# A float32 diffusion step on one core: VectorE's order in the Strassen cycles of the MLPs rewritten, one weight sum stored elsewhere, one strip a product later

## What is computed

```
h = rmsnorm(x, norm_g[layer, 1]) * (1 + sc2) + sh2
x = x + g2 * (jnp.square(jax.nn.relu(h @ mlp_w1[layer])) @ mlp_w2[layer])
```

## Time and profile before

| | |
|---|---|
| median of 3 runs | 1557.08 us (1556.45 to 1558.0) |
| the profiled execution, its own time | 1556.89 us |
| its span | 1555.1 us |
| TensorE (PE) busy | 1518.0 us, 98% |
| weight loads (PEld) | 1477.0 us, 95% |
| VectorE (DVE) | 1139.8 us, 73% |
| ACT | 684.3 us, 44% |
| GpSimd (POOL) | 629.7 us, 40% |
| DMA queue 1 | 159.34 MB, 32.0% of 16 engines' span |

### The profile page before, as it was taken

How to read it: one execution, slowest core, us unless ns; L and a number is a source line. 1 busy time by engine, 2 the same in 40 slices (tenths; PEclk the granted TensorE clock), 3 DMA queues, 4 the chain that set the end, 5 groups by cost and what they waited for, 6 DMA issues and landing times.

```text
span 1555.1 us, 28369 instructions
## 1 busy us (share of the span) xinstructions
PE 1518.0 (98%) x11754; PEld 1477.0 (95%) x11754; DVE 1139.8 (73%) x1877; ACT 684.3 (44%) x1140; POOL 629.7 (40%) x410
## 2 busy tenths in 40 slices
PE   8999999999999999999999999999999999999998
PEld 7999999999999999999999999999999999999998
DVE  5338678675774787887797888773584698889886
ACT  5323333344442354445355434662442355445553
POOL 0233313314322464665574253101333476567641
PEclk9999999999999999999999999999999999999999
DMA  9454334213233334433535122001222212331222
GB/s 328 160 184 149 115 110 130 96 62 109 82 128 119 112 118 162 147 111 123 177 95 162 35 79 65 28 1 55 82 68 68 82 55 73 104 95 55 81 83 82
DMA packets 123168, 162.20 MB, mean 104 GB/s; under 512 B 4640, under 2 KB 87584, under 8 KB 123040
## 3 DMA queue, kind: packets, MB, share of 16 engines
q1 hardware_dynamic: 121808, 159.34, 32.0%
q10 hardware_dynamic: 1232, 1.05, 0.2%
HBM read 156.44 MB, written 3.93 MB: 103 GB/s over the span
## 4 chain that ended last, share of the span: by engine, by line
PE 72%; DVE 15%; ACT 6%; issue 3%; SPq 2%; DMA 2%; POOL 0%; DVEq 0%; ACTq 0%
PE ps L745 42%; PE ps L1169 19%; DVE fx L2602 3%; PE ps L864 3%; PE ps L1417 2%; DVE held L2616 2%; PE ps L1365 1%; ACT wH L1479 1%; DVE fq L2576 1%; DMA ada<-in_ada_w 1%; SPq L573 1%; DVE ps L2106 1%; PE ps L1001 1%; DVE u L2593 1%; PE ps L1034 1%
## 5 line engine op out<-in xcount | busy, mean ns | idle before, releaser
L2031 POOL TENSOR_TENSOR wL<-raw,wH 128x512 fp32r<-128x512 f32 x188 | 288.0, 1558 | 668.2 <-ACT wH L1461 511.2
L1169 PE MATMUL ps<-fx,wH 128*128 128x320 f32 x1120 | 250.6, 312 | 13.5 <-DVE held L2616 8.7
L745 PE MATMUL ps<-hH,wH 128*128 128x320 f32 x704 | 221.1, 314 | 1.9 <-DVE hL L2117 1.3
L745 PE MATMUL ps<-hH,wL 128*128 128x320 f32 x704 | 217.6, 309 | 0.0
L745 PE MATMUL ps<-hL,wH 128*128 128x320 f32 x704 | 217.5, 309 | 0.0
L1169 PEld LDWEIGHTS ps<-fx,wH 128*128 128x128 f32 x1120 | 185.7, 188 | 21.8 <-issue 14.4
L2031 POOL TENSOR_TENSOR wL<-raw_high,wH 128x512 fp32r<-128x512 f32 x100 | 141.8, 1449 | 115.0 <-ACT wH L1461 115.0
L1169 PE MATMUL ps<-fx,wL 128*128 128x320 f32 x560 | 173.1, 309 | 0.0
L745 PE MATMUL ps<-wH,hH 128*128 128x256 f32 x560 | 162.1, 289 | 2.4 <-DVE hL L2117 2.1
L745 PE MATMUL ps<-wL,hH 128*128 128x256 f32 x560 | 158.3, 283 | 0.0
L745 PE MATMUL ps<-wH,hL 128*128 128x256 f32 x560 | 158.3, 283 | 0.0
(11 more groups left out here) (302 smaller groups left out, 3872.6 us busy)
## 6 DMA issues: line engine op xcount, KB each, us to landing
ada<-in_ada_w SPq DMA_DIRECT2D x40, 1024.0 KB, 5.4
raw<-in_mlp_w SPq DMA_DIRECT2D x64, 512.0 KB, 3.7
raw_high<-in_mlp_w SPq DMA_DIRECT2D x64, 512.0 KB, 3.8
raw<-in_even_w_in SPq DMA_DIRECT2D x28, 512.0 KB, 6.1
pre_w<-in_ada_w SPq DMA_DIRECT2D x16, 512.0 KB, 8.9
raw<-in_odd_w_qkv SPq DMA_DIRECT2D x10, 512.0 KB, 3.6
raw<-in_even_w_out SPq DMA_DIRECT2D x8, 512.0 KB, 3.7
raw<-in_odd_w_o SPq DMA_DIRECT2D x6, 512.0 KB, 3.4
```

The lines of the kernel that those rows point to most:

```text
L745: last = nc.tensor.matmul(ps[:, bank, 0:width], a_, b_, start=(k == 0 and p_ == 0), stop=(k == nk - 1 and p_ == 2))
L1169: last = nc.tensor.matmul(ps[:, bank, 0:HALF], a_, b_, start=(opens and k == 0 and p_ == 0), stop=(k == nk - 1 and p_ == 2), skip_group_ch ...
L2031: last = nc.gpsimd.tensor_tensor(wL[:, at % 4, cs], source(key)[:, cs], wH[:, at % 4, cs].bitcast(F32), ALU.subtract)
```

## The change

Nothing is added to or taken from the arithmetic; four things move.

1. `strassen_cycle`: VectorE's list of one cycle in another order.
2. `source`, `wait_raw_free`, `add_blocks`: T4's sum of the first matrix is written over B21's raw buffer instead of `t24_first`. It stands behind `t_lo(s, B21)`, the buffer's next load waits for T4's low part, and the second matrix's T3 sum (into `t24_first`) waits for T2's low part and T4's sum instead of T4's low part.
3. `first_strassen`: the middle strip (`part(1)`) stands behind T1's products instead of T3's.
4. Last cycle: the two row halves of the `mlp_w2` block are loaded in swapped order and `F_AT` follows, so k = 0, 1 are the features of F11 and F21, k = 2, 3 those of F22 and F12.

```diff
@@ F_AT
-    return k % 2 + ((2, 0) if k > 1 else (4, 6))[half]
+    return k % 2 + ((4, 6) if k > 1 else (2, 0))[half]
@@ source
             if key[0] in ("p", "q") and key[2] in (T2, T4):
+                if key[0] == "p" and key[2] == T4:
+                    return raw(key[:2] + (B21,))
                 return (t24_first if key[0] == "p" else t24_second)[:]
@@ wait_raw_free
-            wait_low(engine, *key)
+            wait_low(engine, *(key[:2] + (T4,) if key[0] == "p" and key[2] == B21 else key))
@@ w2
-                        halves = [mlp_w2[layer, 512 * c + 256 * j:512 * c + 256 * (j + 1), 512 * tile:512 * (tile + 1)]
+                        halves = [mlp_w2[layer, 512 * c + 256 * (1 - j):512 * c + 256 * (2 - j), 512 * tile:512 * (tile + 1)]
@@ first_strassen
                     one(T3, S3, 6 + m, m, False)
-                part(1)
                 wait_low(pe, "p", s, T1)
                 pe.wait_ge(dve_free, v)
                 for m in range(2):
                     one(T1, S1, m, m)
+                part(1)
@@ add_blocks
                         if which == "q":
-                            wait_low(dve, "p", WINO * layer_ + n, T4)
+                            wait_low(dve, "p", WINO * layer_ + n, T2)
+                            wait_source(dve, ("p", WINO * layer_ + n, T4))
...
+                    elif which == "p":
+                        wait_low(dve, which, s, B21)
+                        out, a, b, op = b21, b21, t2, ALU.subtract
@@ strassen_cycle
                     t_lo(s, B22)
+                    t_lo(s, B21)
                     p_add(s, T4)
-                    t_lo(s, B21)
+                    q_add(s2, T3)
+                    combine(c, F11, 0)
+                    q_add(s2, T2)
+                    combine(c, F11, 1)
                     t_lo(s, T4)
-                    combine(c, F11, 0)
-                    q_add(s2, T3)
-                    combine(c, F11, 1)
+                    combine(c, F21, 0)
+                    q_add(s2, T1)
+                    combine(c, F21, 1)
+                    operand_lo(c, A11_)
                     modulate(c, 1)
-                    q_add(s2, T2)
-                    combine(c, F21, 0)
-                    operand_lo(c, A11_)
-                    combine(c, F21, 1)
-                    q_add(s2, T1)
                     combine(c, F22, 0)
+                    combine(c, F22, 1)
                     operand_sum(c, S3_)
-                    combine(c, F22, 1)
+                    operand_sum(c, S2_)
                     q_add(s2, T4)
-                    operand_sum(c, S2_)
-                    operand_sum(c, S1_)
                     operand_lo(c, S2_)
...
@@ last_cycle
                     t_lo(s, B22)
-                    p_add(s, T4)
                     held_out(2)
                     t_lo(s, B21)
+                    p_add(s, T4)
                     held_out(3)
```

More of the change, by code:

```diff
@@ L2648, in strassen_cycle @@
                     q_add(s2, T4)
-                    operand_sum(c, S2_)
-                    operand_sum(c, S1_)
                     operand_lo(c, S2_)
-                    product_out(c, 0, 0)
-                    product_out(c, 0, 1)
+                    for m in range(4):
+                        product_out(c, 0, m)
                     operand_lo(c, S3_)
-                    product_out(c, 0, 2)
-                    product_out(c, 0, 3)
-                    product_out(c, 1, 0)
+                    for m in range(3):
+                        product_out(c, 1, m)
@@ L2658, in strassen_cycle @@
                     operand_lo(c, A22_)
-                    product_out(c, 1, 1)
-                    operand_sum(c, S4_)
-                    product_out(c, 1, 2)
                     product_out(c, 1, 3)
                     product_out(c, 2, 0)
-                    operand_lo(c, S1_)
+                    operand_sum(c, S1_)
                     for m in range(1, 4):
                         product_out(c, 2, m)
+                    operand_lo(c, S1_)
+                    operand_sum(c, S4_)
@@ L2667, in strassen_cycle @@
                     product_out(c, 3, 0)
+                    product_out(c, 3, 1)
                     operand_lo(c, S4_)
-                    for m in range(1, 4):
-                        product_out(c, 3, m)
+                    product_out(c, 3, 2)
+                    product_out(c, 3, 3)
                     for m in range(4):
```

## The result

| | before | the change |
|---|---|---|
| median, runs side by side | 1556.78 us (4 runs) | 1546.56 us (4 runs, 1545.89 to 1546.95) |
| ratio | | 0.9932, 95% interval 0.9915 to 0.9950 |
| span of the profiled execution | 1555.1 us | 1544.8 us |
| layer 0, cycles 2 to 6 | 276.4 us | 265.6 us |
| layer 1, cycles 2 to 6 | 257.6 us | 256.8 us |

Forecast were 1544.5 us and a range of 1536.5 to 1553.5. In the spans, layer 0's cycles gave 10.8 us, layer 1's 0.8 us, the stretch between them 0.6 us; the end lost 1.4 us, and the start of cycle 2 came 0.5 us later (537.7 against 537.2, ahead of everything that the change touches). The sum is -10.3 us. One execution of a later kernel (S1's sum back in its old place) took 1830.34 us at a granted clock of 0.75, and is left out of its median.

A forecast was written before the change was run, and what follows sets the result against it. Bound: TensorE, 98% busy, idling mainly on VectorE's order before S2's product. Terms -11.4 - 2.2 + 2.2 - 1.3 + 0.1 = -12.6 us from 1556.89 gave 1544.3, plus 0.2 for the runs' median: 1544.5 us; range 1536.5 to 1553.5.

The forecast's parts named there:

- The S2 wait: TensorE's 1.27 us wait before the first product with S2, held by VectorE's order; claimed to go in all ten cycles.
- The new wait at T2 and T3 in layer 1: TensorE waiting 2.1 us for GpSimd's low parts from layer 1's second cycle on, taking back nearly all the gain there.
- The stretch: VectorE's work from S2's sum to the end of the next cycle's T2 sum: claimed 25.6 us, 23.85 before.
- meetings: Eight places in VectorE's stretch where an instruction waits out a GpSimd instruction: claimed 5.7 us together.
- second meeting of GpSimd's T2 pair: GpSimd's two low-part instructions for T2, now later, also meet VectorE's 1,024-element low part of T1: 1.1 us more.
- The slower rival: VectorE's stretch sets both layers' pace: slower than before from a stretch of 26.7 us on, 1571 us at 28; chance 0.07.
- Layer 1: -2.2 forecast: Cycles 2 to 6 of layer 1: first 49.4 us, four of 51.5, together 255.4 us, or -2.2.
- The last cycle's term (+2.2): Layer 1's last cycle starts with the same new wait for GpSimd's low parts: +2.2 us.
- Layer 0: -11.4 forecast: Cycles 2 to 6 of layer 0: 53.0 us each, 265.0 us instead of 276.4, strip waits included.
- one sign of "Wrong": Waits for `wL` in layer 0, which would show that VectorE's stretch is longer than forecast; no size given.
- the signs of "Right": No S2, strip or `fL` waits; layer 0 cycles 52.9 to 53.3 us; layer 1 49.4, then 51 to 52 with T2/T3 waits.
- The first rival: GpSimd and VectorE sharing the port costs only today's 4.3 us in the stretch, all waits go: 1532.6 us; chance 0.14.

The follow-up runs named there:

- the spaced kernel: The change with VectorE's list respaced, PSUM updates between instructions with both inputs in SBUF, nothing added or removed: 1533.63 us, ratio 0.9850 to the kernel before.

## Why the prediction was right, and where it was off

**The S2 wait: right.** It is gone in all ten cycles, with `held` and `xT`, and what put it there was the order in front of S2's low part: with S1's sum back, 1.25 us of it return in every cycle.

**The new wait at T2 and T3 in layer 1: right in kind, place and total.** "A new wait of 2.1 us at the T2 and T3 products": in cycle 4 the four T2 and T3 products take 9.38 us instead of 4 x 1.76, 2.3 us more. Its parts were not: T2's low part was laid out 2.1 us late and is 1.2, and T3's pair, which was not laid out, is 2.2 late and makes up the rest. That the total agrees is in part luck. The cause is shown by three runs: without GpSimd's low parts beside it, the wait vanishes; with the T3 sum moved by two updates it shrinks, by 0.6 to 0.9 us at T2, as that sum waits 0.80 less; and with the list respaced it vanishes though no work is gone. The Trainium skill (SBUF — State Buffer, "Who interferes with whom") has the rule behind this, an exclusive lock for the whole instruction instead of a split; by that rule, the traces agree, in that instructions on PSUM keep their 0.4 us and a low part issued behind a GpSimd instruction of 1,024 columns takes 3.03.

**The stretch: mis-sized by 0.7 us.** The meetings were "together 5.7 us" and the stretch 25.6, with 0.2 for ACT; measured are 6.6 and 26.3, with none for ACT. All eight meetings are at the places that were laid out, each within 0.3 us. The 1.1 us for a second meeting of GpSimd's T2 pair were on the wrong pair: T2's took 3.48 us, T3's 4.50. The slower rival began at 26.7, so its bound was 0.4 us away.

**Layer 1: -2.2 forecast, -0.8 measured.** The cycles are 0.1 to 0.5 us longer than forecast, by the longer stretch and by a wait that was not laid out: 0.3 us and the 0.1 behind it at the second matrix's B22 products in four of five cycles. It starts at 1366.59 in cycle 4, 0.1 us after the third `xT` update of the six from 1364.99 on is over, the one that frees its PSUM bank. The last cycle's term (+2.2) was 1.4, its "+0.1 for a late combine" 0.7.

**Layer 0: -11.4 forecast, -10.8 measured.** "Some 0.3 us remain" was the margin of T2's low part, and 0.6 us or more did remain. The low part of T3 had no margin of its own in the working, and it is late in cycles 3, 4 and 6 by 0.25 us, with 0.1 behind it. So one sign of "Wrong", waits for `wL` in layer 0, did appear, small and at T3; the signs of "Right" all did, layer 1's first cycle with 49.66 for 49.4. The saving was near but one cause was not: that the strip's waits go was put down to the later strip, and the list without it loses them too.

**The fourth sum at 0: right,** by its own run. **Swapped halves, -0.64 a layer: right** as a price (0.65 in the spaced kernel).

**The first rival, 1532.6 us,** was the time without any new wait. The spaced list comes within 1.1 us of it, by paying 2.9 us in meetings instead of 6.6. **The slower rival** needed 1.1 us more per cycle; GpSimd's instructions of 1,024 columns gave it, but through S2's low part and not through the stretch.

## What to carry to other kernels

Where two engines shut each other out for whole instructions, lay both lists side by side before moving anything: the same sum cost 0.8 or 1.9 us by what the other engine did at that moment. Put the instructions that need no turn (here the PSUM updates) between those that do, about as many as fill one instruction of the other engine; here that was worth 13 us, more than the rest of the change. An engine that is busy for 87% may in truth be waiting inside its instructions, and its free time shows only when the other engine's work is taken away.

## What the runs showed that I had not expected

- Halving GpSimd's instructions hardly helped (1.3 us). VectorE's meetings became shorter, but T2's low part rose from 3.49 to 4.77 us, since GpSimd gave way twice in it and not once.
- The same 1 MB load of a strip's weights took 4.9 to 8.8 us in different cycles and lists. In two cycles of the kernel before that decided whether TensorE waited, and nothing in these runs explains it.
